# Column-tiled modulation products and a second place for part of their loads, in a two-block transformer kernel

## What is computed

```python
c_act = jax.nn.silu(c)                       # one row of 2048
for l in range(2):
    mod = c_act @ w_mod[l] + b_mod[l]        # (1, 2048) @ (2048, 6144)
    shift, scale, gate = jnp.split(mod, 3, axis=-1)
    h = rmsnorm(x, norm_gain[l]) * (1.0 + scale[:, None, :]) + shift[:, None, :]
    proj = h @ w_in[l]                       # (256, 2048) @ (2048, 7504)
    ...                                      # sparse attention and retention
    y = jnp.concatenate([y_a, y_b], axis=-1) @ w_out[l]
    x = x + gate[:, None, :] * y
```

## Time and profile before

| | |
|---|---|
| median of 3 runs | 3424.44 us (3424.09 to 3425.47) |
| the profiled execution | 3421.58 us, of which the trace's span is 3419.8 us |
| PE busy | 2277.9 us, 67% of the span |
| DVE, ACT, POOL busy | 1782.6, 883.7, 728.8 us |
| HBM read | 894.77 MB, mean 262 GB/s |

### The profile page before, as it was taken

How to read it: one execution, slowest core, us unless ns; L and a number is a source line. 1 busy time by engine, 2 the same in 40 slices (tenths; PEclk the granted TensorE clock), 3 DMA queues, 4 the chain that set the end, 5 groups by cost and what they waited for, 6 DMA issues and landing times.

```text
span 3419.8 us, 29641 instructions
## 1 busy us (share of the span) xinstructions
PE 2277.9 (67%) x11714; PEld 1511.5 (44%) x11714; DVE 1782.6 (52%) x2738; ACT 883.7 (26%) x1322; POOL 728.8 (21%) x552
## 2 busy tenths in 40 slices
PE   5799999988999978998988888123223222332235
PEld 1366666567878766665666678100000000000001
DVE  2324546655566765443234557955645555555440
ACT  1123443343455343354353442000000000000000
POOL 1000000000000000000000002555555555555552
PEclk8999999999999999999999999556666666666567
DMA  7787776744655443433232457799999999999998
GB/s 248 249 274 231 248 228 214 237 165 137 179 162 151 144 131 118 151 118 109 95 103 79 155 180 297 306 422 421 421 422 421 422 422 422 422 421 422 422 422 348
DMA packets 268133, 900.92 MB, mean 263 GB/s; under 512 B 20358, under 2 KB 45196, under 8 KB 201548
## 3 DMA queue, kind: packets, MB, share of 16 engines
q0 software_dynamic: 75776, 545.73, 38.7%
q1 hardware_dynamic: 191776, 352.69, 32.6%
q10 hardware_dynamic: 444, 0.61, 0.1%
HBM read 894.77 MB, written 2.10 MB: 262 GB/s over the span
## 4 chain that ended last, share of the span: by engine, by line
PE 53%; DMA 29%; DVE 10%; ACT 4%; issue 2%; POOL 1%; SPq 0%; DVEq 0%; POOLq 0%; ACTq 0%
PE pp L1635 45%; DMA late<-in_peer_v,MI 9%; PE tp L1635 6%; DMA ring<-in_peer_v,MI 4%; DMA P<-in_peer_v,MI 4%; DMA x<-in_peer_v,MI 4%; DVE wL L997 2%; DMA ring<-in_w_mod 2%; DMA SY<-in_peer_v,MI 2%; PE tp L1638 2%; DMA ring<-in_w_in 2%; DVE P L1050 1%; ACT wH L518 1%; DMA ring<-in_peer_w_query 1%; DVE P L1594 0%
## 5 line engine op out<-in xcount | busy, mean ns | idle before, releaser
L997 DVE TENSOR_TENSOR wL<-ring,wH 128x1024 fp32r<-128x1024 f32 (+3 forms) x504 | 581.5, 1160 | 655.2 <-ACT wH L518 654.1
L1635 PE MATMUL pp<-wH,hH 128*128 128x512 f32 (+3 forms) x1888 | 752.3, 398 | 55.9 <-issue 17.4
L1635 PE MATMUL pp<-wL,hH 128*128 128x512 f32 (+3 forms) x1888 | 722.3, 383 | 0.0
L1635 PE MATMUL pp<-wH,hL 128*128 128x512 f32 (+3 forms) x1888 | 722.3, 383 | 0.0
L518 ACT ACTIVATE wH<-ring 128x1024 fp32r<-128x1024 f32 (+3 forms) x504 | 503.6, 1005 | 566.0 <-PE pp L1635 323.8
L1635 PEld LDWEIGHTS pp<-wH,hH 128*128 128x128 f32 x1888 | 362.7, 192 | 251.6 <-issue 134.4
L1635 PE MATMUL pp<-late,S 128*32 128x512 f32 x736 | 231.3, 891 | 292.1 <-DMA SY<-in_peer_v,MI 75.8
L1635 PEld LDWEIGHTS pp<-wH,hL 128*128 128x128 f32 x1888 | 361.8, 192 | 64.2
L1635 PEld LDWEIGHTS pp<-wL,hH 128*128 128x128 f32 x1888 | 363.1, 192 | 55.6 <-issue 0.5
L1635 PE MATMUL pp<-P,S 128*32 128x512 f32 x376 | 271.2, 890 | 150.5 <-DMA late<-in_peer_v,MI 76.6
L1635 PE MATMUL pp<-x,S 128*32 128x512 f32 x376 | 166.9, 882 | 224.7 <-DMA ring<-in_peer_v,MI 224.7
(11 more groups left out here) (296 smaller groups left out, 2989.5 us busy)
## 6 DMA issues: line engine op xcount, KB each, us to landing
ring<-in_w_in SPq DMA_DIRECT2D x288, 512.0 KB, 4.3
ring<-in_w_mod SPq DMA_DIRECT2D x192, 512.0 KB, 4.6
ring<-in_w_out SPq DMA_DIRECT2D x96, 512.0 KB, 4.5
ring<-in_w_in SPq DMA_DIRECT2D x48, 368.0 KB, 3.8
ring<-in_peer_w_query SPq DMA_DIRECT2D x32, 512.0 KB, 4.7
ring<-in_w_in SPq DMA_DIRECT2D x24, 344.0 KB, 3.2
ring<-in_w_in SPq DMA_DIRECT2D x16, 256.0 KB, 3.5
U<-in_dm POOLq DMA_DIRECT2D x8, 384.0 KB, 4.3
```

The source lines that it names most:

```text
L997: tt(lo, raw, hi.bitcast(F32), ALU.subtract).then_inc(*tick("dve_lo", *names))
L1635: return e.matmul(o, l, r, start=start, stop=stop, skip_group_check=skip)
```

## The change

The products of one load now go to the four column positions at once. A load is 128 rows x 1024 columns (also 512 KB, rows of 4 KB), and its one row block meets four slices of 256 columns, each on its own position. A block of 1024 columns takes 16 loads. The bank then holds four different parts of the result, not four partial sums, and two small matmuls with a 4-column selector (`ROW`) turn it.

The loads leave the ring. The first 64 use eight buffers in `late`, memory that `hH` and `hL` take later; the other 128 use two buffers in `P`, where the gate columns of the projection are stored later. In `sync`, load m + 2 is issued in the step of load m and waits for its use (m + 8 in the first 64).

Layer 0's gate and layer 1's shift and scale (blocks 4 to 9, 96 loads) open after group 0 of input projection 0 at a rate of 1.12; layer 1's gate (blocks 10 and 11, 32 loads) opens after group 0 of input projection 2 at a rate of 0.45.

```diff
-    cw[:, ROW] = (i % 32) == 0
+    cw[:, ROW:ROW + 4] = i[:, None] == 32 * np.arange(4)[None, :]
...
-    yield "open", "M", "mods", 0, 0, 8
+    yield "open", "M", "mods", 0, 4
     for k in range(64):
         yield "step", "M"
         if k % 3 == 2:
             yield "step", "X"
     yield "step", "M"
     yield "drain", "X"
-    yield "open", "M", "mods", 0, 8, 12
-    yield "open", "M", "mods", 1, 0, 8
-    yield "open", "M", "mods", 1, 8, 12
...
         def after_in(n):
+            if n == 0:
+                yield ("open", "M", "mods", 10, 12) if l else ("open", "M", "mods", 4, 10)
...
-        yield from project(2 * l, after_in, lambda n: (0.7 if n < 14 else 1.0, 0.6, 1.0))
+        yield from project(2 * l, after_in, lambda n: (0.7 if n < 14 else 1.0, 0.6, 1.12 if l == 0 else 0.45))
...
+        mod_in = [*[late[:, 1024 * b:1024 * b + 1024] for b in range(8)], P[:, 0, GA:GA + 1024], P[:, 1, GA:GA + 1024]]
...
+        def mod_slot(m):
+            if m < 64:
+                return m % 8, m - 8 if m >= 8 else None
+            return 8 + m % 2, m - 2 if m >= 66 and m not in (160, 161) else None
...
     def sync(e, w):
...
+            def mod_load(m):
+                block, k = m // 16, m % 16
+                l, c0 = block // 6, block % 6 * 1024
+                b, before = mod_slot(m)
+                if before is not None:
+                    w.wait_ge(*at("mod used", before))
+                if m in (64, 160):
+                    w.wait_ge(*at("chunk", 0 if m == 64 else 2, 3))
+                e.dma_start(mod_in[b], I["w_mod"][l, k * 128:(k + 1) * 128, c0:c0 + 1024]).then_inc(
+                    *landed(f"mod_in{b}", ("mod", m)))
+
+            def mods(b0, b1):
+                first, last, depth = 16 * b0, 16 * b1, 2 if b0 else 8
+                for m in range(first, first + depth):
+                    mod_load(m)
+                for m in range(first, last):
+                    if m + depth < last:
+                        mod_load(m + depth)
+                    if m % 16 < 15:
+                        yield
+                    elif m + 1 < last:
+                        yield
+                yield
...
     def scalar(e, w):
...
+                            else:
+                                w.wait_ge(*at("mod used", 191 if p else 159))
                             act(P[:, t, c:c + wd], bank, ACT.Exp, scale=-1.0).then_inc(
...
-                    act(msum[:, :], side_bank[:, :], ACT.Copy).then_inc(*tick("act_side", ("side out", s)))
+                    act(msum[:, 0:256], side_bank[:, 0:256], ACT.Copy).then_inc(*tick("act_side", ("side out", n)))
...
     def tensor(e, w):
...
-                        for k in range(2):
-                            kk = 2 * pc + k
-                            o = 32 * (kk % 4)
-                            m = mm(side_bank[o:o + 32, :], cact[:, kk:kk + 1].to_broadcast([128, 32]), wv[:, k, :], kk < 4, kk >= 12)
-                        m.then_inc(*tick("pe_side", ("ring used", r), *([("side", s)] if pc == 7 else [])))
+                        w.wait_ge(*at("mod", m))
+                        for g in range(4):
+                            z = mm(side_bank[32 * g:32 * g + 32, 0:256], cact[:, k:k + 1].to_broadcast([128, 32]),
+                                   wv[:, 256 * g:256 * g + 256], k == 0, k == 15)
+                        z.then_inc(*tick("pe_side", ("mod used", m), *([("side", n)] if k == 15 else [])))
...
-                    for b in range(4):
-                        m = mm(pr[:, b:b + 1], msum[:, b * 128:(b + 1) * 128], CW[:, ROW:ROW + 1], True, True)
-                    m.then_inc(*tick("pe_turned", ("turned", u), ("side read", s)))
+                    for b in range(2):
+                        z = mm(pr[:, 4 * b:4 * b + 4], msum[:, b * 128:(b + 1) * 128], CW[:, ROW:ROW + 4], True, True)
+                    z.then_inc(*tick("pe_turned", ("turned", u), ("side read", n)))
```

More of the change, by code:

```diff
@@ L334, in mixer_peer_program @@
         mcol = sb("mcol", [128, 2, 48])
-        mrow = sb("mrow", [128, 48])
         msum = sb("msum", [128, 512])
@@ L361, in mixer_peer_program @@
                      "dve_lo", "dve_stored", "dve_x", "dve_y", "dve_h", "dve_side",
-                     "const_in", "pos_in", "x_in", "meta_in", "forget_in", "ffn_in", "decay_in", "turned_in", "out_done",
+                     *[f"mod_in{i}" for i in range(10)], "const_in", "pos_in", "x_in", "meta_in", "forget_in", "ffn_in", "decay_in", "turned_in", "out_done",
                      *[f"ring_in{i}" for i in range(NS)], *[f"expert_in{i}" for i in range(NG)]):
@@ L617, in tables, with mods @@
                             yield
[L619 to L623, removed]
-                            yield
[L625 to L628, removed]
-                    act(msum[:, :], side_bank[:, :], ACT.Copy).then_inc(*tick("act_side", ("side out", s)))
+            def mods(b0, b1):
+                for block in range(b0, b1):
+                    for k in range(16):
+                        if k < 15:
+                            yield
+                    n = next(side)
+                    w.wait_ge(*at("side", n))
+                    if n:
+                        w.wait_ge(*at("side read", n - 1))
+                    act(msum[:, 0:256], side_bank[:, 0:256], ACT.Copy).then_inc(*tick("act_side", ("side out", n)))
                     yield
@@ L1149, in mods @@
                     u = next(turn)
+                    l, k0 = block // 6, block % 6 * 8
+                    mc = mcol[:, l, k0:k0 + 8]
                     w.wait_ge(*at("turned", u))
[L1151 to L1160, removed]
+                    tt(mc.rearrange("p (g b) -> p b g", g=4), heads(tp[u % 2][:, 0:8], 2),
+                       bcol[:, l * 48 + k0:l * 48 + k0 + 8].rearrange("p (g b) -> p b g", g=4), ALU.add).then_inc(
+                        *tick("dve_side", ("pair free", u)))
+                    if block % 6 in (2, 3):
+                        w.wait_ge(*now("dve_side"))
+                        ts(mc, mc, 1.0, None, ALU.add, None).then_inc(*tick("dve_side"))
+                        w.wait_ge(*now("dve_side"))
+                        tt(mc, mc, col("norm_gain", 16 * l + k0 - 16, 8), ALU.mult).then_inc(*tick("dve_side"))
             def meta_sum(p, n):
@@ L1731, in tables, with mods @@
                             yield
[L1733 to L1740, removed]
-                            w.wait_ge(*at("c ready"))
-                            if s:
-                                w.wait_ge(*at("side out", s - 1))
-                        for k in range(2):
-                            kk = 2 * pc + k
-                            o = 32 * (kk % 4)
-                            m = mm(side_bank[o:o + 32, :], cact[:, kk:kk + 1].to_broadcast([128, 32]), wv[:, k, :], kk < 4, kk >= 12)
-                        m.then_inc(*tick("pe_side", ("ring used", r), *([("side", s)] if pc == 7 else [])))
-                        if pc < 7:
+            def mods(b0, b1):
+                for block in range(b0, b1):
+                    n = next(side)
+                    for k in range(16):
+                        m = 16 * block + k
+                        wv = mod_in[mod_slot(m)[0]]
+                        if k == 0:
+                            w.wait_ge(*at("c ready"))
+                            if n:
+                                w.wait_ge(*at("side out", n - 1))
+                        w.wait_ge(*at("mod", m))
[3 more added lines that the diff above has]
+                        z.then_inc(*tick("pe_side", ("mod used", m), *([("side", n)] if k == 15 else [])))
+                        if k < 15:
@@ L1750, in mods @@
                             yield
                     yield
-                    w.wait_ge(*at("side out", s))
+                    w.wait_ge(*at("side out", n))
                     pr, u = pair()
-                    for b in range(4):
-                        m = mm(pr[:, b:b + 1], msum[:, b * 128:(b + 1) * 128], CW[:, ROW:ROW + 1], True, True)
-                    m.then_inc(*tick("pe_turned", ("turned", u), ("side read", s)))
+                    for b in range(2):
+                        z = mm(pr[:, 4 * b:4 * b + 4], msum[:, b * 128:(b + 1) * 128], CW[:, ROW:ROW + 4], True, True)
```

## The result

The changed kernel takes 3482.44 us (median of 4 runs, 3471.23 to 3488.08) against 3424.77 us: a ratio of 1.0164, 95% interval 1.0139 to 1.0190. It is slower by 58 us, where 37 us faster was forecast; the time lies outside the range, 25 us beyond the rival that ended slower. Its runs also spread over 17 us; those of before over 1.4 here and over 5 to 10 beside the experiments. The profiled execution took 3488.08 us, its span is 3486.2.

What follows compares the result with a forecast made beforehand. Loads of `w_mod` were taken to rule stage A and PE to bound stage B, with late splits lengthening C. The terms -33 (A), -50 (B) and +46 (C) gave -37 us against 3424.4: 3388 us, range 3345 to 3435.

Steps and rivals of the forecast that it cites:

- The products: PE's M steps: four column positions of 256 columns take 0.77 us in place of 1.19, saving 0.42 a step.
- Stage A: Before input projection 0, 0 to 153 us: eight loads in flight in place of four, -33 us (-20 to -38).
- PE alone: Stages B and C counted by PE's work only, without late splits: -69.5 us in B, +26 in C.
- B: Input projection 0, 563.0 us before the change: forecast -50 us.
- C: Input projection 2, 422.4 us before the change, which gets 32 M steps: forecast +46 us, upper end +85.
- the loop: SP to split load to ACT, DVE and PE, over three pieces: piece q + 3 starts at least 7.5 us after step q.
- the late splits: Split loads behind SP's wait for the current M step: two pieces remain from that step's end to their use.
- I take twice that, 0.25: Groups 4 to 11 of B: PE idle 0.25 us a piece, twice the earlier 0.13, 16 us in 64 pieces.
- the 0.15 of groups 4 to 9 of C: Exposed wait of 0.15 us for each of 48 pieces; with 17 us of steps and turns, 24 us.
- rival 1: Stages B and C: ACT and DVE absorb the late splits, only PE's work counts; 3347 us, chance 0.22.
- 5 us of slack: Groups 4 to 11 of B: some 5 us ACT and DVE had for lane work, nearly gone after the change.
- rival 2: Stages B and C: every lane step behind a late split, 4.9 us a piece in B; slower, 3457 us, chance 0.20.

Runs made afterwards that it cites:

- experiment 4: The kernel before with the new products alone, loads still through the ring and 128 of them beside input projection 0: 3365.71 us, ratio 0.9822.
- experiment 3: Experiment 1 with four in place of eight buffers (and loads in flight) for the first 64 loads: 3374.55 us, ratio 0.9849.
- Experiment 1: The changed kernel, but beside the projections SP issues load m, not load m + 2, in the step of load m: 3345.50 us, ratio 0.9768.
- experiment 9: The changed kernel, lockstep kept, with each split load of projections 0 to 3 issued two splits earlier: 3357.78 us, ratio 0.9804.
- experiment 6: The changed kernel with lane M at 1.0 in place of 1.12 steps a piece beside input projection 0: 3465.74 us, ratio 1.0111.
- experiment 8: Experiment 1, but beside input projection 2 load m + 2 is again issued in the step of load m: 3402.19 us, ratio 0.9922.

## Why the prediction was wrong

**The products: right.** The changed kernel's step at full clock (timeline of PE):

```profile
161.57 0.33 PE L1655 MATMUL pp<-wH,hH 128*128 128x368 f32 x1
161.73 0.33 PE L1655 MATMUL pp<-wL,hH 128*128 128x368 f32 x1
161.90 0.33 PE L1655 MATMUL pp<-wH,hL 128*128 128x368 f32 x1
162.16 0.64 PE L1655 MATMUL pp<-P,cact 128*32 128x256 f32 x8
162.72 0.43 PE L1655 MATMUL pp<-wH,hH 128*128 128x368 f32 x1
163.00 0.33 PE L1655 MATMUL pp<-wL,hH 128*128 128x368 f32 x1
```

From 161.90 to 163.00 is 1.10, of which two ordinary starts are 0.33: 0.77 us, as forecast from the earlier trace rows; it is the median of 66 such steps in experiment 4 too. The prediction read the 8 columns as if they spoke against a cost for each instruction. They do not, with 0.36 us for eight of them; it is the 0.77 that leaves no room for 0.1 us more.

**Stage A: right in sum**, 119.0 for 152.9. But I booked all of it to the buffers; experiment 3 gives them 23 us.

**PE alone: not so close.** The forecast had 493.5 us for B and 448.4 for C without the loop. Experiment 1 has 509.8 and 443.4. Against the 16 us missing in B stand 14.7 that PE waits there for modulation loads, a wait that the sum did not have.

**What failed: the price of the late splits.** The prediction saw the wait, the queue behind it and the loop. The step that failed is its choice between the bounds: "I take twice that, 0.25", 16 us in groups 4 to 11 of B, and the 0.15 of groups 4 to 9 of C. Measured against experiment 1, groups 4 to 11 lose 68 us in B (338.9 against 270.4; 1.07 a piece) and 29 in C. Groups 1 to 3, where the loop was counted, lose 14 in B and 24 in C. In all 40 us were booked for the late splits, the difference of the forecast to rival 1, and they cost 137. The row I scaled from, PE's 0.13 us of idle a piece in the earlier trace rows, was taken with 5 us of slack, by the prediction's own estimate. What a queue costs with slack said nothing here of what it costs with almost none. The nearer bound was rival 2's 4.9 us a piece, 314 us for groups 4 to 11.

They took 339. Of the 68 us, PE was idle for 42 more (47.5 for 5.0) and busy for 26 more (291.4 for 265.4), with 1594 instructions in both kernels. PE's longest waits in these groups of the changed kernel:

```profile
PE tp L1658 <- ACT S L727: 11.6, 3, 4.9
PE pp L1655 <- DVE wL L1018: 7.7, 7, 2.7
PE tp L1655 <- ACT msum L650: 6.5, 2, 4.8
```

With the smaller rows, 28 of the 47 us are lane steps and turns (`tp`) held by ACT or DVE, 14 are pieces held by them, 5 are modulation loads. That is rival 2's mechanism: the lanes' steps on ACT and DVE stand behind a late split, and PE behind them.

**The term that was missing: the clock.** The 26 us of busy time go with a granted clock of 0.92 for 0.99. After some of the waits what follows runs at half clock, as the 4.44 and 2.90 us for the same 20 instructions show. Summed from the starts of the first and last matmul of each piece, the 64 pieces' own matmuls took 192.6 us against 169.0 in experiment 1; 7 of these 24 us are four pauses inside a piece, where PE waits for ACT, the rest slower starts. In groups 1 to 3 of C the chain of waits has two pieces and a step in 6.44 us (this kernel, issue to issue 13.2 us, four pieces):

```profile
845.34 0.33 SPq L479
...
845.72 4.55 DMA ring<-in_w_in
...
850.29 0.82 ACT wH L538
...
851.13 0.94 DVE wL L1018
...
852.12 6.44 PE pp L1655 x32
...
858.57 0.34 SPq L479
```

At full clock they are 2 x 2.02 + 0.77 = 4.8; the window 852.12 to 858.56 has a granted clock of 0.74. So a turn is 3.3 us a piece, where 2.75 was taken, and the stage's three groups take 75.8 us for a forecast 66. In groups 1 to 3 of B, 95.1 us for 72, the clock is little of it: PE is busy for 70.4 us, for 68.6 in experiment 1. There one lane step waits 7.3 us for DVE, PE waits 10.2 us for `wL` and 4.0 for modulation loads; what each is worth was not taken apart. That the clock causes its share, and is not only found beside the waits, was argued from these rows; no run kept PE busy in the waits to isolate it.

**Rival 2 was the nearest**, with 0.20, and its 3457 us lies 25 below the median. It did not miss by one term. By the trace B's groups 4 to 11 are 25 us above its sum (+46 for +21) and groups 1 to 3 23 above (+16.5 for -6.5); C is 9 below (+76 for +85: it charged 63 us for groups 4 to 9, and groups 4 to 11 grew by 40). Its rule from the Trainium skill ("DMA: Bandwidth & Descriptors", Rules for kernel authors), to issue a DMA early and wait for it late, agrees with the runs where one load is looked at: stage A gained 23 us by it, and experiments 1 and 9 obey it for the split loads. Experiment 1 does so by issuing the modulation loads later, so the rule did not say which of two loads in one queue to favour.

**Rival 1**, which I gave 0.22, put 3347 us on the kernel without late splits; experiment 1 measured 3345.5. That is in part luck: B came out 16 us above its sum, C 5 below, and all else 9 below, where nothing was booked. In every kernel with the new products the part after input projection 2 takes 2165 to 2169 us, for 2173.9 before; no run says why.

## What to carry to other kernels

In an engine's queue a wait is paid by what stands behind it. Count the lead of those instructions, in loop turns, before and after, and ask whether the path from their issue to their use still fits; a loop that just fitted on average (3.9 us for 4.16 here) did not fit once other work shared the engines in it, so take the price at zero slack, not the one seen with slack. Where a load must wait for a buffer, issue it at the last place that still meets its own use, so that nothing else is held. Where stalls recur, price some of the work after them at half clock, and look at the granted clock to see how much: it was 26 of 68 us in one stretch here and 2 of 14 in another.

## What the runs showed of the hardware

- Eight float32 instructions of 256 columns on four column positions add 0.77 us between matmuls, four of 512 on two positions 1.19; both consume one load of 512 KB.
- With eight loads of 512 KB in flight in stage A a load takes 9.2 us to land (median) and a 2 MB load beside them 13.1 us, for 10.3 beside four (experiment 3) and 9.5 before; still the stage is 23 us shorter than with four.
- The three kernels in lockstep (the changed one, experiments 6 and 8) spread over 17, 13 and 17 us in four runs each, the others over 4 to 12, and the kernel before over 1 to 10. Whether the loop of loads is the reason was not tested.
- The granted clock was 0.92 over the 339 us of groups 4 to 11 of B, where PE stood idle for 47.5 us in waits of up to 4.9 us, and 0.99 to 1.00 in the same groups of both stages before and in experiment 1, where it idled for 8 us or less.
